# ACT counts the three widest score tiles in the last 12 search rounds of a top-k threshold

## The chip, the cores and the metric

The kernel runs on one core of a Trainium2 chip. The metric is the time of one execution on the device in microseconds (us), for which the slowest core counts; here there is one. The engines are PE (TensorE: matmuls, with PEld for its weight loads), DVE (VectorE), ACT (ScalarE), POOL (GpSimd) and SP (SyncE, which issues the DMAs). Each works through its own queue in the order in which the program wrote it, and they meet at semaphores only.

## What is computed

Two layers of a hybrid trunk, for 1024 prompt tokens and 64 sample tokens. A layer normalises x, projects it through one matrix into all branches, runs a gated linear recurrence (A), a sparse attention (B) and a differential attention (C), gates each, and projects the result back. The change touches how B picks its keys:

```python
s_idx = relu(einsum('bqhd,bkd->bqhk', qi, kidx) * IDX_DIM ** -0.5)
score = einsum('bqhk,bqh->bqk', s_idx, w) * IDX_HEADS ** -0.5
score = where(mask, score, -inf)
top_val, top_idx = top_k(score, 256)        # of up to 1088 keys
# attention B then runs over these 256 keys alone
```

The kernel never sorts. For each query it searches, bit by bit, for the float32 value that at least 256 scores reach, and masks what lies below it.

## The kernel before

Queries are tiled by 128: tiles 0 to 7 are the prompt, tile 8 (SAMPLE) the 64 sample tokens. Prompt tile t sees 128 (t + 1) keys, the sample tile 1088. Tiles 0 and 1 have at most 256 keys and need no selection, so seven tiles are scored (SCORED): 384, 512, 640, 768, 896 and 1024 keys on 128 partitions, and 1088 keys on 64.

A layer has two stages. In the **front**, PE transposes x and runs the input projection in the order of the list FRONT (written by `front()`); it makes the index scores early, and ends with the token-row groups ("tm"): four units (bv, bg, cv, cg) of five groups each, four of the five for 256 tokens and the last for 64, so 20 groups numbered 0 to 19 below. ACT walks the same list and drains every group from PSUM into r_vg (`rows_out`, L1013). The groups use four PSUM banks in turn: PE may fill group n only when group n - 4 has been drained. In the **attention** stage PE, DVE and ACT walk the list STEPS: for each tile and head PE makes scores (L1507 to L1517), DVE reduces them to their maximum (L1298), ACT takes the exponential (L1046), and so on, with two PSUM slots for score maps. The first tile in attention is tile 2, the second the sample tile.

While PE works on the front, DVE does the selection. It has the scores of all seven tiles in SBUF (r_sc), starts from the sign, and then does 31 rounds, one per bit, in `search` (L1225): `count` (L1209) compares each tile with its candidate threshold `cb` and adds up how many scores reach it, one instruction of seven per tile, with the comparison written to r_ix as a by-product; then one small instruction turns the seven counts into a correction (L1229) and one makes the next candidate (L1232, in the last round L1235). The rounds are cut in three pieces of 6, 2 and 23 (SPLITS), with work of the recurrence between them. After round 30 DVE selects: it counts strictly above the threshold (L1268), and then takes four instructions per tile to handle ties and write the mask (L1278 to L1281). The last of them releases `sel_ready`.

Two things wait for that. DVE itself starts with attention only behind it, in its own queue. ACT waits for all seven `sel_ready` (L1034) between its last drain and its first exponential, since the exponentials overwrite r_sc.

Of the kernel before, what the change touches and what calls it, by code (L numbers as in the profile page):

```python
# [6 lines left out]
P = 128  # L7
# [5 lines left out]
SAMPLE = NT - 1  # L13
# [11 lines left out]
TOPK = 256  # L25
# [9 lines left out]
UNITS = ["iq", "ik", "ax0", "ax1", "cq", "bq", "ag0", "ag1", "ck", "bk", "bv", "bg", "cv", "cg"]  # L35
# [28 lines left out]
TMG = [(0, 2), (2, 4), (4, 6), (6, 8), (8, 9)]  # L64
# [11 lines left out]
ORDER = [2, SAMPLE, 3, 0, 1, 4, 5, 6, 7]  # L76
BITS = 31
SPLITS = [6, 2, BITS - 8]


FIRST_PROJ = 3
# [59 lines left out]
def front():  # L141

    def mm(u, s, p):
        return [("mm", u, s, p, k) for k in range(KT)]

    steps = [("xt", 0), ("xt", 1), ("xt", 2)] + mm("iq", 0, 0) + [("xt", 3)] + mm("iq", 1, 0)
    steps += [("xt", 4), ("xt", 5)] + mm("iq", 0, 1) + [("xt", 6), ("xt", 7), ("xt", 8)] + mm("iq", 1, 1)
    steps += mm("iq", 0, 2) + mm("iq", 1, 2)
    for p in range(3):
        steps += mm("ik", 0, p)  # L150

    def after_piece(done):
# [24 lines left out]
    steps.append(("ixr",))  # L177
    todo += [k for u in UNITS[6:10] for s in range(2) for p in range(3) for k in mm(u, s, p)]
    done = 0
    for k in todo:  # L180
        steps.append(k)
        if k[4] < KT - 1:
            continue
        done += 1
        steps += after_piece(done)
    for u in UNITS[10:]:
        for g in range(len(TMG)):
            steps.append(("tm", u, g))
    return steps


# [19 lines left out]
def build(nc, x0, w_in, acst, gate_w, npost, w_out, ckT, kidxT, vcache,  # L211
          y, o_k, o_ik, o_v, o_conv, o_h):
    f32, bf16, i32, u16 = mybir.dt.float32, mybir.dt.bfloat16, mybir.dt.int32, mybir.dt.uint16
    ALU = mybir.AluOpType
# [4 lines left out]
    with ctx:  # L219
# [117 lines left out]
        lamp = sm[:, 216:217]  # L337
        v, smask, cb, kb = smi[:, 0:7], smi[:, 7:14], smi[:, 14:21], smi[:, 21:28]
        bits = sb("bits", 32, i32)
        lamjunk = sb("lamjunk", CHALF)  # L340
        sub2 = sb("sub2", DC)

# [44 lines left out]
        u_ready, h_ready, ya_ready = sem("u_ready"), sem("h_ready"), sem("ya_ready")  # L387
        hl_ready = sem("hl_ready")
        sel_ready = sem("sel_ready")
        lam_s, lam_e, lam_ready = sem("lam_s"), sem("lam_e"), sem("lam_ready")  # L390
        negm_ready, comb_ready = sem("negm_ready"), sem("comb_ready")
        yh_ready, y_ready = sem("yh_ready"), sem("y_ready")
# [168 lines left out]
        for layer in range(DEPTH):  # L561
            x_from = y if layer else x0
            with nc.Block() as block:  # L563
# [315 lines left out]
                def _(act):  # L879
# [122 lines left out]
                    def rows_out(u, g):  # L1002
# [9 lines left out]
                        fn = ACT.Silu if u[1] == "g" else ACT.Copy  # L1012
                        drains_ring(nc.scalar.activation(vg[0:r, t0:t1, c:c + BW], src, fn), key)  # L1013

                    n = 0
                    for s in FRONT:
                        if s[0] == "mm" and s[4] == KT - 1:
                            evac_fm(s[1], s[2], s[3])
                        elif s[0] == "root":
                            act.wait_ge(m2_ready, AJ)  # L1020
                            nc.scalar.activation(tall, tall, ACT.Sqrt, scale=-1.0).then_inc(root_ready, 1)
                        elif s[0] == "iw":
                            weights_out()
                        elif s[0] == "iqs":
                            stack_out(s[1], s[2])
                        elif s[0] in ("ix", "ixr"):
                            relu_out(s, n)
                            n += 1
                        elif s[0] == "ga":
                            gate_out(s[1], s[2], s[3])  # L1030
                        elif s[0] == "tm":
                            rows_out(s[1], s[2])

                    act.wait_ge(sel_ready, len(SCORED))  # L1034
                    nmap = 0
# [39 lines left out]
                def _(dve):  # L1075
                    steps = [0]

                    def link(ins):
                        steps[0] += 1
                        ins.then_inc(dve_step, 1)  # L1080
                        dve.wait_ge(dve_step, steps[0])
# [124 lines left out]

                    def count(bound, last_inc):  # L1209
                        for c, t in enumerate(SCORED):  # L1210
                            b = bound if isinstance(bound, float) else bound[0:rows(t), c:c + 1]
                            ins = vec.tensor_scalar(unsel[t][0:rows(t), :], sc[t][0:rows(t), :], b, None,  # L1212
                                                    ALU.is_ge, ALU.add, accum_out=cnt[0:rows(t), c:c + 1])
                        return ins

                    dve.wait_ge(ik_stored, 16)
# [1 line left out]
                    vec.memset(unsel[SAMPLE][NSA:P, :], 0.0)  # L1218
                    dve.wait_ge(bits_made, 2)
                    link(vec.memset(v, 0))  # L1220
                    link(count(0.0, None))
                    link(vec.tensor_scalar(smask, cnt, float(TOPK), -1.0, ALU.is_lt, ALU.mult))
                    link(vec.scalar_tensor_tensor(cb, v, bits[:, 0:1], smask, ALU.bitwise_or, ALU.bitwise_xor))

                    def search(first, rounds):  # L1225

                        for b in range(first, first + rounds):
                            link(count(cb.bitcast(f32), None))
                            link(vec.tensor_scalar(kb, cnt, float(TOPK), float(2 ** (BITS - 1 - b)),  # L1229
                                                   ALU.is_lt, ALU.mult))  # L1230
                            if b + 1 < BITS:
                                link(vec.scalar_tensor_tensor(cb, kb, bits[:, b + 1:b + 2], cb,  # L1232
                                                              ALU.bitwise_or, ALU.bitwise_xor))
                            else:
                                link(vec.tensor_tensor(cb, cb, kb, ALU.bitwise_xor))  # L1235

                    search(0, SPLITS[0])
                    dve.wait_ge(decay_done, AJ)
# [21 lines left out]
                        vec.tensor_copy(hl[:, j, 0:1], tw[j][:, NPR - 1:NPR])  # L1260
                        ins = vec.tensor_copy(hl[:, j, 1:2], tw[j][:, ACW - 1:ACW])
                    ins.then_inc(hl_ready, 1)
                    search(SPLITS[0] + SPLITS[1], SPLITS[2])

                    thr = cb.bitcast(f32)
                    for c, t in enumerate(SCORED):
# [407 lines left out]
```

## Time and profile before

| | |
|---|---|
| time, median of 3 runs | 1833.22 us (1826.09 to 1840.75) |
| the profiled execution: its own time | 1831.72 us |
| span of its trace | 1829.9 us |
| granted clock of PE, mean over the span | 0.954 |
| busy: PE, DVE, ACT, POOL | 92%, 66%, 31%, 23% of the span |

The span runs from the first to the last instruction of the trace. Layer 0 fills its first half and layer 1 the second; the same work stands 911.2 us later in layer 1. In each layer, the front takes about 487 us from the layer's start and attention the rest. The rows further down are of three kinds: a timeline (start, duration, engine, line, operation, and in brackets how long the engine was idle before it and who released it), groups (all instructions of one line and shape, with count, busy us and mean ns), and windows (how long each engine was busy in a stretch).

### The profile page before, as it was taken

What the parts mean: (1) busy time and instruction counts of PE and PEld (TensorE: products, weight loads), DVE (VectorE), ACT (ScalarE), POOL (GpSimd) and SP (SyncE); (2) the same over time, 40 slices, a digit from 0 to 9 for tenths busy, and PEclk for the clock granted to TensorE, in tenths of its full rate; (3) what the DMA queues carried; (4) which work ended last, traced back from release to release, by engine and by line L of the source; (5) the groups of instructions that cost most, each with busy time, mean ns of one, the idle gap of its engine ahead of it and who ended that gap; (6) DMA issues with size and microseconds to landing.
All of it is one profiled execution on the core that took longest, in us unless ns stands there. A gap on an engine that the chain in (4) does not pass through costs nothing. (4 is left out here: it accounts for less than half of the span.)

```text
span 1829.9 us, 21077 instructions
## 1 busy us (share of the span) xinstructions
PE 1679.8 (92%) x7330; PEld 1125.0 (61%) x7330; DVE 1213.0 (66%) x2510; ACT 568.9 (31%) x1111; POOL 424.6 (23%) x535
## 2 busy tenths in 40 slices
PE   6999999999888989999779999999999888899997
PEld 4566666688745456666345666666887444566663
DVE  3378999999655355565033799999995543456650
ACT  2276421200233223333022864212002332333330
POOL 2001523410022343231110024234000223433211
PEclk9999999999989989999879999999998899899998
DMA  5100001310222021110051000113103120211100
GB/s 163 50 24 24 23 25 60 105 54 24 96 80 104 29 58 35 35 35 24 35 164 49 23 24 23 46 51 94 52 24 127 50 104 29 59 35 35 35 24 35
DMA packets 39177, 99.18 MB, mean 54 GB/s; under 512 B 8673, under 2 KB 27617, under 8 KB 34721
## 3 DMA queue, kind: packets, MB, share of 16 engines
q1 hardware_dynamic: 39072, 97.85, 16.2%
q8 instruction: 59, 0.97, 0.2%
q14 instruction: 46, 0.37, 0.1%
HBM read 66.84 MB, written 18.14 MB: 46 GB/s over the span
## 5 line engine op out<-in xcount | busy, mean ns | idle before, releaser
L1377 PE MATMUL ps<-r_xn,r_w 128*128 128x384 f32 (+1 forms) x1824 | 589.9, 476 | 12.9 <-issue 8.3
L1377 PEld LDWEIGHTS ps<-r_xn,r_w 128*128 128x128 f32 x1824 | 347.3, 192 | 209.9 <-issue 23.2
L1212 DVE TENSOR_SCALAR_CACHE_REDUCE r_ix<-r_sc,smi 128x384 bf16<-128x384 f32 x434 | 405.4, 998 | 2.1
L1298 DVE TENSOR_REDUCE sm<-ps 128x1 f32<-128x384 f32 (+8 forms) x216 | 171.6, 810 | 163.5 <-PE ps L1517 85.9
L1046 ACT ACTIVATE r_sc<-ps,sm 128x384 f32<-128x384 f32 (+8 forms) x216 | 169.8, 787 | 343.8 <-DVE sm L1298 343.3
L1444 PE MATMUL ps<-r_w,r_xn 128*128 128x256 f32 (+1 forms) x1152 | 251.3, 380 | 0.0
L1444 PEld LDWEIGHTS ps<-r_w,r_xn 128*128 128x128 f32 (+1 forms) x1152 | 210.9, 184 | 40.1 <-issue 5.0
L1548 PE MATMUL ps<-r_vg,r_w 128*128 128x64 f32 (+1 forms) x1184 | 162.9, 284 | 26.0 <-DVE r_w L554 14.8
L1548 PEld LDWEIGHTS ps<-r_vg,r_w 128*128 128x128 f32 (+1 forms) x1184 | 151.2, 200 | 35.9 <-DVE r_w L517 21.2
L1531 PE MATMUL ps<-ident,r_sc 128*128 128x128 f32 (+1 forms) x720 | 121.9, 280 | 41.1 <-ACT r_w L517 17.1
L1580 PE MATMUL ps<-r_xn,r_ag 128*128 128x512 f32 (+1 forms) x288 | 146.6, 656 | 8.6 <-DVE r_res L1319 6.1
L1531 PEld LDWEIGHTS ps<-ident,r_sc 128*128 128x128 f32 (+1 forms) x720 | 85.8, 151 | 84.2 <-issue 32.6
L1580 PE MATMUL ps<-r_xn,r_vg 128*128 128x512 f32 (+1 forms) x288 | 130.7, 596 | 0.0
L554 DVE TENSOR_SCALAR r_w<-ps,sm 128x64 f32<-128x64 f32 (+1 forms) x144 | 40.1, 279 | 133.0 <-PE ps L1548 131.8
L1175 DVE SCALAR_TENSOR_TENSOR r_sc<-r_vg,sm,r_sc 128x384 f32<-128x384 f32 (+6 forms) x98 | 97.8, 998 | 30.6 <-ACT r_vg L977 25.0
L1580 PEld LDWEIGHTS ps<-r_xn,r_ag 128*128 128x128 f32 (+1 forms) x288 | 56.3, 205 | 73.6 <-issue 66.7
L977 ACT ACTIVATE r_vg<-ps 128x384 f32<-128x384 f32 (+6 forms) x112 | 88.5, 796 | 31.6 <-PE ps L1414 26.3
L1013 ACT ACTIVATE r_vg<-ps 128x512 f32<-128x512 f32 (+1 forms) x40 | 22.1, 553 | 227.0 <-PE ps L1444 227.0
L517 DVE COPY r_w<-ps 128x512 f32<-128x512 f32 (+3 forms) x112 | 59.7, 533 | 43.7 <-PE ps L1531 42.9
L1511 PE MATMUL ps<-kst_c,qc_hi 128*128 128x512 f32 (+3 forms) x192 | 81.0, 422 | 8.1 <-ACT r_sc L1046 6.5
L1580 PEld LDWEIGHTS ps<-r_xn,r_vg 128*128 128x128 f32 (+1 forms) x288 | 51.3, 185 | 57.5 <-issue 57.2
L517 ACT COPY r_w<-ps 128x512 f32<-128x512 f32 (+3 forms) x112 | 51.6, 461 | 106.7 <-PE ps L1531 106.5
(188 smaller groups left out, 1976.2 us busy)
## 6 DMA issues: line engine op xcount, KB each, us to landing
r_w<-w_in SPq DMA_DIRECT2D x28, 1024.0 KB, 4.9
r_xn<-w_out SPq DMA_DIRECT2D x2, 4096.0 KB, 13.5
y<-r_res SPq DMA_DIRECT2D x16, 512.0 KB, 2.9
r_vg<-x SPq DMA_DIRECT2D x8, 512.0 KB, 9.9
r_xn<-ckT SPq DMA_DIRECT2D x2, 2048.0 KB, 8.4
r_xn<-vcache SPq DMA_DIRECT2D x2, 2048.0 KB, 14.1
o_v<-r_vg SPq DMA_DIRECT2D x4, 1024.0 KB, 11.1
r_sc<-x SPq DMA_DIRECT2D x8, 512.0 KB, 4.4
```

What stands on the lines that cost most here:

```text
L517: ins = copy(pT[i % 2][:, k0:k1, 0:r], src[:, 0:k1 - k0, 0:r])
L977: drains_x(nc.scalar.activation(dst, src, ACT.Relu, scale=scale), key)
L1046: ins = nc.scalar.activation(ex[2 * (i % 2) + m][0:r, 0:w], on_slot(s, w, r), ACT.Exp, bias=negm[0:r, c:c + 1], accum_out=den[0:r, c:c + 1])
L1175: ins = vec.scalar_tensor_tensor(sc[t][0:r, 0:w], src, iw[0:r, t, h:h + 1], sc[t][0:r, 0:w], ALU.mult, ALU.add)
L1212: ins = vec.tensor_scalar(unsel[t][0:rows(t), :], sc[t][0:rows(t), :], b, None, ALU.is_ge, ALU.add, accum_out=cnt[0:rows(t), c:c + 1])
L1298: vec.tensor_reduce(negm[0:r, c:c + 1], on_slot(s, w, r), X, ALU.max, negate=True)\
L1377: ins = nc.tensor.matmul(on_ring(key, cn), w[:, k, P * s + at:P * (s + 1) + at], xnT[:, k, c0:c0 + cn], start=(k == 0), stop=(k == KT - 1))
L1444: ins = nc.tensor.matmul(on_ring(key)[0:rows(t), BW * (t - t0):BW * (t - t0 + 1)], xnT[:, k, P * t:P * t + rows(t)], w[:, k, :], start=(k ...
L1511: ins = nc.tensor.matmul(out, q, kst[kind][:, h, c0:c0 + cn], start=(n2 == 0), stop=(n2 == 1 and not more))
L1531: ins = nc.tensor.transpose(tbank[0:kn, P * (k - 4 * g):P * (k - 4 * g) + r], ex[2 * (i % 2)][0:r, P * k:P * k + kn], ident[0:r, 0:r])
L1548: ins = nc.tensor.matmul(obank[0:r, :], pT[i % 2][0:kn, k, 0:r], vals, start=(k == 0), stop=(k == nk - 1))
L1580: ins = nc.tensor.matmul(mixb[0:r, part // 2, :], yk, wo[:, k, c0:c0 + BANK], start=(k == 0), stop=(k == KT - 1))
```

## The change

In the last 12 rounds (SHARED; rounds 19 to 30) DVE counts only four tiles, those of 384 to 768 keys, and ACT counts the other three (896, 1024 and 1088 keys) with a Sign activation of (candidate - score) whose accumulated output is the number below minus the number above. `limit` holds, for each tile, the bound to which its count is compared. A round now goes to and fro: DVE writes the candidate and raises `cand_ready`; ACT does three passes and raises `act_counted`; DVE, behind its own four counts, waits for them, and makes the next candidate with three small instructions in place of two. Where a score equals the candidate, a sign counts as zero, so ACT's result can be off by one step; `settle` repairs that for the three tiles, once, after round 30: nine small instructions, one exact count of the three tiles on DVE, seven small instructions. The small instructions work on three or six columns.

Where ACT does its counts is set in the list FRONT: `COUNTS_AT` names for each of the 12 shared rounds the token-row group behind whose drain its count stands. One constant table more is filled ahead of the search (11 instructions on DVE with a few columns each), and one copy of the candidates onto themselves raises `cand_ready` for the first time.

```diff
+SHARED = 12
+ACT_TILES = [6, 7, SAMPLE]
+DVE_TILES = [t for t in SCORED if t not in ACT_TILES]
+COUNTS_AT = [5, 6, 7, 7, 8, 9, 9, 10, 11, 11, 12, 13]
...
-    for u in UNITS[10:]:
-        for g in range(len(TMG)):
-            steps.append(("tm", u, g))
+    for n, (u, g) in enumerate([(u, g) for u in UNITS[10:] for g in range(len(TMG))]):
+        steps.append(("tm", u, g))
+        steps += [("count", b) for b, at in enumerate(COUNTS_AT) if at == n]
...
+                    def count_out(b):
+
+                        act.wait_ge(cand_ready, b + 1)
+                        for t in ACT_TILES:
+                            c, r = SCORED.index(t), rows(t)
+                            nc.scalar.activation(unsel[t][0:r, :], sc[t][0:r, :], ACT.Sign, scale=-1.0,
+                                                 bias=cb.bitcast(f32)[0:r, c:c + 1],
+                                                 accum_out=cnt[0:r, c:c + 1]).then_inc(act_counted, 1)
...
+                    def search_shared(first, rounds):
+
+                        for n in range(rounds):
+                            b = first + n
+                            following = float(2 ** (BITS - 2 - b)) if b + 1 < BITS else 0.0
+                            link(count(cb.bitcast(f32), DVE_TILES, ALU.is_lt))
+                            dve.wait_ge(act_counted, len(ACT_TILES) * (n + 1))
+                            link(vec.tensor_tensor(kbf, cnt, limit, ALU.is_gt))
+                            link(vec.tensor_scalar(kb, kbf, float(2 ** (BITS - 1 - b)), following,
+                                                   ALU.mult, ALU.add))
+                            ins = vec.tensor_tensor(cb, cb, kb, ALU.bitwise_xor)
+                            if n + 1 < rounds:
+                                ins.then_inc(cand_ready, 1)
+                                dve.wait_ge(cand_ready, n + 2)
+                            else:
+                                link(ins)
...
+                        link(vec.tensor_tensor(two, high, low, ALU.bitwise_or))
+                        link(vec.tensor_tensor(cb[:, ND:NS], two, sa, ALU.bitwise_xor))
+                        link(count(cb.bitcast(f32), ACT_TILES))
+                        link(vec.tensor_scalar(ca, cnt[:, ND:NS], float(TOPK), -1.0, ALU.is_ge, ALU.mult))
...
-                    search(SPLITS[0] + SPLITS[1], SPLITS[2])
+                    search(SPLITS[0] + SPLITS[1], SPLITS[2] - SHARED)
+                    vec.tensor_tensor(cb, cb, cb, ALU.bitwise_or).then_inc(cand_ready, 1)
+                    dve.wait_ge(cand_ready, 1)
+                    search_shared(BITS - SHARED, SHARED)
+                    settle()
```

**On ACT**, at the drains of token-row groups 4 to 8 of layer 0 (r_vg is where they go, the semaphores in brackets are what each instruction waits for), the queue was, before:

```order
L1013 ACTIVATE r_vg<-ps 64x256 [waits ring_filled1]
L1013 ACTIVATE r_vg<-ps 128x2x256 [waits ring_filled2]
L1013 ACTIVATE r_vg<-ps 128x2x256 [waits ring_filled3]
L1013 ACTIVATE r_vg<-ps 128x2x256 [waits ring_filled0]
L1013 ACTIVATE r_vg<-ps 128x2x256 [waits ring_filled1]
```

Now the first of these places, with the drains of groups 4, 5 and 6:

```order
L1024 ACTIVATE r_vg<-ps 64x256 [waits ring_filled1]
L1024 ACTIVATE r_vg<-ps 128x2x256 [waits ring_filled2]
L1031 ACTIVATE r_ix,sm<-r_sc,smi 128x896 [waits cand_ready]
L1031 ACTIVATE r_ix,sm<-r_sc,smi 128x1024
L1031 ACTIVATE r_ix,sm<-r_sc,smi 64x1088
L1024 ACTIVATE r_vg<-ps 128x2x256 [waits ring_filled3]
```

and the last, from the drain of group 12 (the first row) over that of group 13 (the fifth) to that of group 14:

```order
L1024 ACTIVATE r_vg<-ps 128x2x256 [waits ring_filled1]
L1031 ACTIVATE r_ix,sm<-r_sc,smi 128x896 [waits cand_ready]
L1031 ACTIVATE r_ix,sm<-r_sc,smi 128x1024
L1031 ACTIVATE r_ix,sm<-r_sc,smi 64x1088
L1024 ACTIVATE r_vg<-ps 128x2x256 [waits ring_filled2]
L1031 ACTIVATE r_ix,sm<-r_sc,smi 128x896 [waits cand_ready]
L1031 ACTIVATE r_ix,sm<-r_sc,smi 128x1024
L1031 ACTIVATE r_ix,sm<-r_sc,smi 64x1088
L1024 ACTIVATE r_vg<-ps 64x256 [waits ring_filled3]
```

Between one drain and the next ACT now has one or two counts of three passes each; the first stands behind group 5, the last behind group 13. No instruction between them loads an activation table.

**On DVE**, round 30 and the first instruction of the selection were, before:

```order
L1212 TENSOR_SCALAR r_ix,sm<-r_sc,smi 128x384 [waits dve_step]
L1212 TENSOR_SCALAR r_ix,sm<-r_sc,smi 128x512
L1212 TENSOR_SCALAR r_ix,sm<-r_sc,smi 128x640
L1212 TENSOR_SCALAR r_ix,sm<-r_sc,smi 128x768
L1212 TENSOR_SCALAR r_ix,sm<-r_sc,smi 128x896
L1212 TENSOR_SCALAR r_ix,sm<-r_sc,smi 128x1024
L1212 TENSOR_SCALAR r_ix,sm<-r_sc,smi 64x1088
L1229 TENSOR_SCALAR smi<-sm 128x7 [waits dve_step]
L1235 TENSOR_TENSOR smi<-smi 128x7 [waits dve_step]
L1268 TENSOR_SCALAR r_ix,sm<-r_sc,smi 128x384 [waits dve_step]
```

Now round 30 (its candidate was made by the first row) and the first instruction of the repair are:

```order
L1276 TENSOR_TENSOR smi<-smi 128x7 [waits dve_step]
L1235 TENSOR_SCALAR r_ix,sm<-r_sc,smi 128x384 [waits cand_ready]
L1235 TENSOR_SCALAR r_ix,sm<-r_sc,smi 128x512
L1235 TENSOR_SCALAR r_ix,sm<-r_sc,smi 128x640
L1235 TENSOR_SCALAR r_ix,sm<-r_sc,smi 128x768
L1273 TENSOR_TENSOR sm<-sm 128x7 [waits act_counted,dve_step]
L1274 TENSOR_SCALAR smi<-sm 128x7 [waits dve_step]
L1276 TENSOR_TENSOR smi<-smi 128x7 [waits dve_step]
```

and the repair's count with what stands around it, up to the last small instruction but one ahead of the selection, is:

```order
L1294 ISA sm<-sm 128x6 [waits dve_step]
L1295 TENSOR_TENSOR sm<-sm 128x3 [waits dve_step]
L1296 TENSOR_TENSOR smi<-sm,smi 128x3 [waits dve_step]
L1235 TENSOR_SCALAR r_ix,sm<-r_sc,smi 128x896 [waits dve_step]
L1235 TENSOR_SCALAR r_ix,sm<-r_sc,smi 128x1024
L1235 TENSOR_SCALAR r_ix,sm<-r_sc,smi 64x1088
L1298 TENSOR_SCALAR sm<-sm 128x3 [waits dve_step]
L1299 TENSOR_TENSOR sm<-sm,smi 128x3 [waits dve_step]
L1300 TENSOR_TENSOR sm<-sm 128x3 [waits dve_step]
L1301 TENSOR_TENSOR smi<-smi,sm 128x3 [waits dve_step]
L1302 TENSOR_SCALAR sm<-smi 128x3 [waits dve_step]
L1303 TENSOR_TENSOR smi<-smi,sm 128x3 [waits dve_step]
```

Three counts have left the round; one wait for ACT (`act_counted`) has come into it, and 16 small instructions with one count of three tiles stand between the last round and the selection.

## Rows read from the trace of the kernel before

**Rows 1.** The page, busy us, share and instructions of each engine.

```profile
PE 1679.8 (92%) x7330; PEld 1125.0 (61%) x7330; DVE 1213.0 (66%) x2510; ACT 568.9 (31%) x1111; POOL 424.6 (23%) x535
```

**Rows 2.** Timeline, layer 0: start us, us, engine, line, op [idle before].

```profile
475.82 1.34 DVE L1281 SCALAR_TENSOR_TENSOR r_ix<-r_sc,smi,r_ix 64x1088 bf16<-64x1088 f32 x1
...
487.26 0.41 PE L1511 MATMUL ps<-kst_c,qc_hi 128*128 128x384 f32 x1 [0.76 <-issue]
...
488.02 1.02 DVE L1298 TENSOR_REDUCE sm<-ps 128x1 f32<-128x384 f32 x2 [10.85 <-PE ps L1517]
...
488.65 1.28 ACT L1046 ACT_TABLE_LOAD   x1 [1.74 <-DVE sm L1298]
```

**Rows 3.** Timeline, layer 1, the same places: a V/G drain, DVE's first attention reduce.

```profile
1310.59 0.60 ACT L1013 ACTIVATE r_vg<-ps 128x512 f32<-128x512 f32 x1 [6.73 <-PE ps L1444]
...
1399.21 1.02 DVE L1298 TENSOR_REDUCE sm<-ps 128x1 f32<-128x384 f32 x2 [10.83 <-PE ps L1517]
```

**Rows 4.** Timeline of DVE, layer 0: search rounds, start of the selection.

```profile
353.05 0.61 DVE L1212 TENSOR_SCALAR_CACHE_REDUCE r_ix<-r_sc,smi 128x384 bf16<-128x384 f32 x1
...
427.76 1.14 DVE L1212 TENSOR_SCALAR_CACHE_REDUCE r_ix<-r_sc,smi 128x896 bf16<-128x896 f32 x1
...
431.40 0.17 DVE L1229 TENSOR_SCALAR smi<-sm 128x7 int32<-128x7 f32 x1
...
438.65 0.17 DVE L1235 TENSOR_TENSOR smi<-smi 128x7 int32<-128x7 int32 x1
438.86 0.61 DVE L1268 TENSOR_SCALAR_CACHE_REDUCE r_ix<-r_sc,smi 128x384 bf16<-128x384 f32 x1
```

**Rows 5.** Timeline of ACT, layer 0: drains of three token-row groups.

```profile
399.38 0.60 ACT L1013 ACTIVATE r_vg<-ps 128x512 f32<-128x512 f32 x1 [6.73 <-PE ps L1444]
...
413.19 0.60 ACT L1013 ACTIVATE r_vg<-ps 128x512 f32<-128x512 f32 x1 [6.31 <-PE ps L1444]
...
451.52 0.60 ACT L1013 ACTIVATE r_vg<-ps 128x512 f32<-128x512 f32 x1 [6.31 <-PE ps L1444]
```

**Rows 6.** Groups by line and form: passes of ACT, busy us, mean ns.

```profile
L1046 ACT ACTIVATE r_sc<-ps,sm 64x1088 f32<-64x1088 f32 x24 | 27.9, 1163 | 69.0 <-DVE sm L1298 69.0
L1046 ACT ACTIVATE r_sc<-ps,sm 128x1024 f32<-128x1024 f32 x24 | 26.8, 1115 | 45.2 <-DVE sm L1298 45.2
L1046 ACT ACTIVATE r_sc<-ps,sm 128x896 f32<-128x896 f32 x24 | 24.1, 1008 | 41.6 <-DVE sm L1298 41.6
...
L998 ACT ACTIVATE r_ax<-r_vg,sm 128x1091 f32<-128x1091 f32 x8 | 9.6, 1206 | 0.1
```

**Rows 7.** Timeline of ACT: one pass, its accumulator read, the next pass.

```profile
540.06 1.16 ACT L1046 ACTIVATE r_sc<-ps,sm 64x1088 f32<-64x1088 f32 x1 [0.58 <-DVE sm L1298]
541.12 0.19 ACT L1046 ACTIVATION_READ_ACCUMULATOR r_sc<-ps,sm 64x1 f32 x1
541.22 0.35 ACT L517 COPY r_w<-ps 128x256 f32<-128x256 f32 x1
```

**Rows 8.** Timeline: a DVE reduce and the ACT pass that waits for it.

```profile
502.64 0.55 DVE L1298 TENSOR_REDUCE sm<-ps 128x1 f32<-128x384 f32 x1
...
503.23 0.58 ACT L1046 ACTIVATE r_sc<-ps,sm 128x384 f32<-128x384 f32 x1 [1.42 <-DVE sm L1298]
```

**Rows 9.** Windows: us, busy PE, PEld, DVE, ACT, POOL, PEclk, DMA share, GB/s.

```profile
488.00:500.00 12.00, 8.53 (x40) 6.11 (x39) 7.11 (x22) 5.84 (x15) 1.44 (x2) 0.72 0.77 285
```

**Rows 10.** Timeline of PE inside that window: one score matmul.

```profile
495.93 0.67 PE L1511 MATMUL ps<-kst_c,qc_hi 128*128 128x384 f32 x1
```

**Rows 11.** Sample tile: issue of its cached values, landing (us last), first matmuls.

```profile
491.33 0.44 SPq L642 DMA_DIRECT2D r_xn<-vcache  x1
...
r_xn<-vcache SPq DMA_DIRECT2D x1, 2048.0 KB, 14.1
...
509.71 1.93 PE L1507 MATMUL ps<-r_xn,r_res 128*64 128x512 f32 x4
```

More of the change, by code:

```diff
@@ L78 @@
 SPLITS = [6, 2, BITS - 8]
+SHARED = 12
+ACT_TILES = [6, 7, SAMPLE]
+DVE_TILES = [t for t in SCORED if t not in ACT_TILES]
+ND = len(DVE_TILES)
+NS = len(SCORED)
+COUNTS_AT = [5, 6, 7, 7, 8, 9, 9, 10, 11, 11, 12, 13]
 FIRST_PROJ = 3
@@ L339, in build @@
         bits = sb("bits", 32, i32)
+        limit, kbf, maskf = sm[:, 224:231], sm[:, 231:238], sm[:, 238:241]
+        sti, maski = sm[:, 241:256].bitcast(i32), smi[:, 28:31]
         lamjunk = sb("lamjunk", CHALF)
@@ L389, in build @@
         sel_ready = sem("sel_ready")
+        cand_ready, act_counted = sem("cand_ready"), sem("act_counted")
         lam_s, lam_e, lam_ready = sem("lam_s"), sem("lam_e"), sem("lam_ready")
@@ L1032, in _ @@
                             rows_out(s[1], s[2])
+                        elif s[0] == "count":
+                            count_out(s[1])
                     act.wait_ge(sel_ready, len(SCORED))
@@ L1205, in _, with count @@
                             vec.memset(sc[t][0:64, width(t) - 64:width(t)], LOWEST)
-                    def count(bound, last_inc):
-                        for c, t in enumerate(SCORED):
+                    def count(bound, tiles, op=ALU.is_ge):
+                        for t in tiles:
+                            c = SCORED.index(t)
                             b = bound if isinstance(bound, float) else bound[0:rows(t), c:c + 1]
                             ins = vec.tensor_scalar(unsel[t][0:rows(t), :], sc[t][0:rows(t), :], b, None,
-                                                    ALU.is_ge, ALU.add, accum_out=cnt[0:rows(t), c:c + 1])
+                                                    op, ALU.add, accum_out=cnt[0:rows(t), c:c + 1])
                         return ins
@@ L1220, in _ @@
                     link(vec.memset(v, 0))
-                    link(count(0.0, None))
+                    for c, t in enumerate(SCORED):
+                        vec.memset(limit[:, c:c + 1], float(width(t) - TOPK * (2 if t in ACT_TILES else 1)))
+                    vec.memset(maskf[:, 0:1], 65535.0)
+                    vec.memset(maskf[:, 1:2], 2147418112.0)
+                    link(vec.memset(maskf[:, 2:3], 65536.0))
+                    link(vec.tensor_copy(maski, maskf))
+                    link(count(0.0, SCORED))
                     link(vec.tensor_scalar(smask, cnt, float(TOPK), -1.0, ALU.is_lt, ALU.mult))
@@ L1227, in search @@
                         for b in range(first, first + rounds):
-                            link(count(cb.bitcast(f32), None))
+                            link(count(cb.bitcast(f32), SCORED))
                             link(vec.tensor_scalar(kb, cnt, float(TOPK), float(2 ** (BITS - 1 - b)),
@@ new lines, in settle @@
+                    def settle():
+                        va, sa = v[:, ND:NS], smask[:, ND:NS]
+                        low, high, one, two, ca = (sti[:, 3 * q:3 * q + 3] for q in range(5))
+                        m16, mhi, carry = (maski[:, q:q + 1].to_broadcast([P, 3]) for q in range(3))
+                        link(vec.tensor_tensor(va, cb[:, ND:NS], sa, ALU.bitwise_xor))
+                        link(vec.tensor_tensor(low, va, m16, ALU.bitwise_and))
+                        link(vec.tensor_scalar(low, low, 1.0, None, ALU.add))
+                        link(vec.tensor_tensor(one, low, carry, ALU.bitwise_and))
+                        link(vec.tensor_tensor(low, low, m16, ALU.bitwise_and))
+                        link(vec.tensor_tensor(high, va, mhi, ALU.bitwise_and))
+                        link(vec.tensor_tensor(high, high, one, ALU.add))
+                        link(vec.tensor_tensor(two, high, low, ALU.bitwise_or))
+                        link(vec.tensor_tensor(cb[:, ND:NS], two, sa, ALU.bitwise_xor))
+                        link(count(cb.bitcast(f32), ACT_TILES))
+                        link(vec.tensor_scalar(ca, cnt[:, ND:NS], float(TOPK), -1.0, ALU.is_ge, ALU.mult))
+                        link(vec.tensor_tensor(two, two, va, ALU.bitwise_xor))
+                        link(vec.tensor_tensor(two, two, ca, ALU.bitwise_and))
+                        link(vec.tensor_tensor(va, va, two, ALU.bitwise_xor))
+                        link(vec.tensor_scalar(ca, va, 8388608.0, -1.0, ALU.is_ge, ALU.mult))
+                        link(vec.tensor_tensor(va, va, ca, ALU.bitwise_and))
+                        link(vec.tensor_tensor(cb[:, ND:NS], va, sa, ALU.bitwise_xor))
```

## The prediction

> **What bounds the kernel now.** I read the page first, then the timeline where the front hands over to attention, since the change touches only DVE and ACT in the front. PE is busy for 92% of the span, DVE for 66% [rows 1]. At the hand-over of layer 0 the last instruction of the selection starts at 475.82 and takes 1.34, so DVE is done at 477.16. It then stands idle for 10.85 us: its next work, the first reduce of attention, starts at 488.02, and what released it was PE, which had made its first attention matmul at 487.26 [rows 2]. Layer 1 shows the same with 10.83 us of idleness [rows 3]. So the front ends with PE's last projection group, and the whole search on DVE is hidden behind it, with 10.8 us to spare. A faster search is worth nothing here; a search that ends more than 10.8 us later is paid for in full, because DVE starts attention only behind its selection and ACT's exponentials wait for it too.
>
> **Where the time of a round goes now.** A round is 7.05 us: round 29's first small instruction starts at 431.40, and round 30's 0.21 ahead of its second at 438.65, so at 438.44; the search ends with the latter, and the selection's first count starts at 438.86 [rows 4]. Twelve rounds back, round 19 begins at 353.05 [rows 4]; that is a little more than 12 x 7.05 = 84.6 us before 438.86, since one round on the way was longer. The three tiles that leave DVE are what lies between 427.76 and 431.40, 3.64 us; the four that stay take about 3.0.
>
> **When ACT can count.** This is the step that decides. ACT has time (31% busy), but it works in order, and the first count stands behind the drain of token-row group 5. That drain starts at 399.38, when PE has finished the group [rows 5]. DVE asks for the first count at 353.05 + about 0.2. So DVE does its four tiles by 356.3 and then waits for ACT until about 403.5: some 47 us of idleness, in which the old kernel did more than six rounds. All that the sharing can give back, 12 x (7.05 - 4.2) = 34 us, is less than that.
>
> **The pace from there.** One shared round is ACT's three passes plus the reply. ACT's passes over PSUM with a pointer bias and an accumulator take 1.008, 1.115 and 1.163 us for 896, 1024 and 1088 columns [rows 6]. The new ones read SBUF: the nearest row is L998 with 1.206 us for 1091 columns, 0.04 more than the PSUM form, so I take 1.05 + 1.155 + 1.20 = 3.40. A pass and its successor follow without a gap, and the last accumulator read ends 0.09 behind the pass (541.31 against 541.22) [rows 7]: 3.5 us. A signal from DVE to ACT costs 0.04 (502.64 + 0.55 to 503.23) [rows 8], and I take the same back. DVE's three small instructions are 0.21 each (438.65 to 438.86) [rows 4], 0.6 in all. A round is then 3.5 + 0.6 + 0.08 = 4.2 us. DVE's own 3.0 us lie beside ACT's 3.5. ACT's drains, 0.60 each, fall in the 0.7 us in which it waits for DVE, so they cost nothing; without that cover it would be 0.6 us for each of the six drains on the way.
>
> The counts of rounds 19 to 21 stand alone behind groups 5 to 7, which are 6.9 us apart, so they wait for PE. From the drain of group 7 (413.19 + 0.60 = 413.8) [rows 5] on, rounds chain: round 21's count starts there, round 29's eight rounds later, at 413.8 + 8 x 4.2 = 447.4, and round 30's could at 451.6. It stands behind the drain of group 13, which starts at 451.52 and ends at 452.1 [rows 5]. So the last count runs from 452.1 to 455.6 and the last round ends at 456.3: 17.5 us later than the 438.8 of now. PE isn't held up: no drain is more than about 2 us late, and PE needs a bank again only four groups later. The 11 instructions of the constant table, at most 0.2 us each, delay DVE ahead of a wait of 47 us, and cost nothing.
>
> **The repair and the sum.** `settle` has 16 small instructions at 0.21, 3.4 us, and one count of three tiles, 3.64: 7.0 us, all on the path, since nothing else is on DVE. The selection behind it is unchanged and takes 477.16 - 438.86 = 38.3 us. It ends at 456.3 + 7.0 + 38.3 = 501.6, against 477.16: 24.5 us later. The cover takes 10.85 of it, so attention starts 13.65 us later. On top comes PE's clock. In the window from 488 to 500, after 2 us of idleness, the granted clock is 0.72 on average [rows 9], and a score matmul takes 0.67 us at the lower of the two levels (1.2 GHz) where it took 0.41 at the higher one (2.4 GHz) [rows 10, 2]. With 13 us more of idleness the first maps are made at 1.2 GHz for longer. Eight maps of the first C heads with two such matmuls each would be 4 us if all were exposed; below is nothing, if DVE and ACT hide them. I take 1. In all 14.7 us for a layer, 29 for two, and 1831.7 + 29.3 = 1861 us by the profiled execution's own time, which lies 1.5 us under the median. I predict 1861 us, 1.5% slower.
>
> The Trainium skill speaks against the move itself: "ScalarE: Activation LUTs", section "Rules for kernel authors", would leave simple elementwise work to VectorE, which it calls up to about three times faster per element in bf16. The rows do not show that for this counting: DVE takes 1.14 us for 896 columns [rows 4] and ACT 1.05, so the sum above does not use it. By the rule, with three times DVE's time for the three tiles, a round would be 11.6 us and the kernel about 190 us slower (rival 3).
>
> The same page, section "Table sets: the hidden batching unit", has a function outside the active set cost a table load at each change; the trace has such a load, 1.28 us, ahead of the first exponential [rows 2]. The order of the changed kernel has none between drains and counts, and no term stands for it.
>
> **The rivals.**
> 1. *ACT's place in its queue sets the end of the search* (the forecast): 0.74. 1851 to 1874 us.
> 2. *The round trip is longer than I think.* With the chain of rounds from 413.8 on, each 0.1 us more of a round costs 0.9 us a layer once it passes 4.26. With signals of 0.3 us in place of 0.04, passes of 1.3 us and drains that are not hidden a round would be 5.1 us: the search ends 9 x 5.1 + 0.6 + 3.9 us after 413.8, at 464, and the kernel is at 1831.7 + 2 x (14.7 + 8) = 1877. For it: no row shows an accumulating pass from SBUF with a pointer bias, nor a semaphore that goes to and fro. Against: the rows of both halves are short. 0.14.
> 3. *ACT is far slower per element* than its other passes, as by the rule above: At three times the 3.64 us that DVE takes now for the three tiles a round is 10.9 + 0.7 = 11.6 us, and the 12 rounds chain from 400.0 to 539: 100 us later than now, 96 with the repair and the cover, 2025 us; at twice ACT's 3.4 it is 1930 us. Rows 6 speak against both. 0.02.
> 4. *The cover is enough after all, no change.* The selection would have to end by 488.0, so that the last round ended by 442.7 and ACT's last count began by 438.5. That needs group 13 finished 13 us earlier, or its count not behind it. The order of ACT's queue excludes the second, and PE is busy throughout the first. What could bring it back is something later that waits today for what is not the chain. The sample tile is the first candidate: its cached values are issued at 491.33 and land 14.1 us later, at 505.4, and its first matmuls run at 509.71 with no idleness ahead of them [rows 11]. If that transfer was felt through its traffic, a start 13.7 us later would run undisturbed; I see 4 us of margin and no wait. 1833 us, 0.07.
> 5. *Faster.* The other side: attention gets its 13.7 us back and more, because the transfers (77% DMA share in the window at 488 [rows 9]) are done before it starts, where they slowed it before. It decides only if they cost attention more than 14.7 us a layer, while that window is 12 us long with DVE busy for 7.1. About 1820 us. 0.03.
>
> **How the numbers follow.** The point is that of case 1. The range takes in case 1, with the clock's term from 0 to 4 us a layer and the runs' own spread (1826 to 1841), and reaches to case 2: 1851 to 1877 us. About 1% is what a measurement of this kernel can tell from no change. Slower by over 1% is above 1851.5: nearly all of case 1, and cases 2 and 3, 0.89. Within 1%: 0.08, case 4 and a little of case 1. Faster: 0.03.
>
> **What would show it.** In the changed profile DVE should stand idle for about 47 us in each layer once, behind the four counts of round 19, released by ACT's L1031, and for 2.5 to 3 us in rounds 20 and 21. The rounds from 413.8 on should follow every 4.2 us; if they come every 5, case 2 holds. The last Sign pass should start right behind the drain of group 13, near 452. The first reduce of attention should follow the selection at once, near 501.7, with DVE no longer waiting for PE, and PE idle from 488 to about 504 in its place. PE's projection groups should end at 487 as before; if they end later, drains have held them up, which I exclude. The forecast is wrong if the first reduce starts before 495, or if attention behind it is more than 5 us a layer shorter or longer than before.

## The result: 1.4% slower

| | median us | runs |
|---|---|---|
| before | 1833.04 | 4 (1826.09 to 1840.75) |
| changed | 1857.97 | 4 (1851.01 to 1863.08) |
| ratio | 1.0144 | 95% interval 1.009 to 1.0198 |

The forecast was 1861 us. The profiled execution of the changed kernel took 1851.01 us, the fastest of its four, with a span of 1849.2 us against 1829.9 before.

The page of the changed kernel (busy us, share, instructions), which answers to [rows 1]: ACT has gained 80 us, DVE has lost 69, and the span has grown all the same.

```profile
PE 1674.1 (91%) x7330; PEld 1122.0 (61%) x7330; DVE 1144.2 (62%) x2458; ACT 649.2 (35%) x1255; POOL 427.0 (23%) x535
```

DVE in layer 0 of the changed kernel, timeline (start us, us, engine, line, operation, idleness before it and who ended it). L1273 is the first small instruction of a shared round, L1288 the first of the repair, L1341 the selection's first count, L1354 its last instruction, L1371 the first reduce of attention. It answers to [rows 2] and [rows 4].

```profile
401.57 0.17 DVE L1273 TENSOR_TENSOR sm<-sm 128x7 f32<-128x7 f32 x1 [47.15 <-ACT r_ix L1031]
...
408.48 0.17 DVE L1273 TENSOR_TENSOR sm<-sm 128x7 f32<-128x7 f32 x1 [3.27 <-ACT r_ix L1031]
...
419.55 0.17 DVE L1273 TENSOR_TENSOR sm<-sm 128x7 f32<-128x7 f32 x1 [0.54 <-ACT r_ix L1031]
...
448.69 0.17 DVE L1273 TENSOR_TENSOR sm<-sm 128x7 f32<-128x7 f32 x1 [0.53 <-ACT r_ix L1031]
...
453.71 0.17 DVE L1273 TENSOR_TENSOR sm<-sm 128x7 f32<-128x7 f32 x1 [1.40 <-ACT r_ix L1031]
...
454.32 0.16 DVE L1288 TENSOR_TENSOR smi<-smi 128x3 int32<-128x3 int32 x1
...
461.14 0.61 DVE L1341 TENSOR_SCALAR_CACHE_REDUCE r_ix<-r_sc,smi 128x384 bf16<-128x384 f32 x1
...
498.95 1.34 DVE L1354 SCALAR_TENSOR_TENSOR r_ix<-r_sc,smi,r_ix 64x1088 bf16<-64x1088 f32 x1
500.33 1.02 DVE L1371 TENSOR_REDUCE sm<-ps 128x1 f32<-128x384 f32 x2
```

The whole course stands here. DVE is idle for 47.15 us (46.07 in layer 1) before it can finish the first shared round, waiting for ACT. In rounds 20 and 21 it waits for 3.3 us, in the eight after them for 0.53 each, and in the last for 1.40. The last round ends at 454.3, the repair at 461.1, the selection at 500.3, and the reduce of attention follows at once, with no idleness ahead of it, where DVE waited for 10.85 us before [rows 2].

ACT in the same layer, timeline: L1024 are drains (groups 5, 13 and 19), L1031 the passes of the new counts, and ACTIVATION_READ_ACCUMULATOR what each pass has behind it. It answers to [rows 5] and [rows 6].

```profile
397.54 0.60 ACT L1024 ACTIVATE r_vg<-ps 128x512 f32<-128x512 f32 x1 [6.73 <-PE ps L1517]
398.03 1.03 ACT L1031 ACTIVATE r_ix<-r_sc,smi 128x896 bf16<-128x896 f32 x1
...
399.06 1.14 ACT L1031 ACTIVATE r_ix<-r_sc,smi 128x1024 bf16<-128x1024 f32 x1
...
400.19 1.19 ACT L1031 ACTIVATE r_ix<-r_sc,smi 64x1088 bf16<-64x1088 f32 x1
401.28 0.19 ACT L1031 ACTIVATION_READ_ACCUMULATOR r_ix<-r_sc,smi 64x1 f32 x1
...
449.68 0.60 ACT L1024 ACTIVATE r_vg<-ps 128x512 f32<-128x512 f32 x1 [1.09 <-PE ps L1517]
450.17 1.03 ACT L1031 ACTIVATE r_ix<-r_sc,smi 128x896 bf16<-128x896 f32 x1
...
484.70 0.38 ACT L1024 ACTIVATE r_vg<-ps 64x256 f32<-64x256 f32 x1 [3.00 <-PE ps L1517]
```

ACT drained group 5 at 397.54 and began its first count within that drain's end; the last count starts behind the drain of group 13. This execution's front ran 1.84 us ahead of the one before (last drain 484.70 against 486.54), so every absolute time of layer 0 is to be read with 1.84 us added: the first reduce at 500.33 answers to 502.17, and the forecast said 501.7.

PE, timeline: the first matmul of attention, and the first that had to wait for an exponential.

```profile
485.42 0.42 PE L1584 MATMUL ps<-kst_c,qc_hi 128*128 128x384 f32 x1 [0.76 <-issue]
...
502.99 0.69 PE L1584 MATMUL ps<-kst_c,qc_hi 128*128 128x384 f32 x1 [16.44 <-ACT r_sc L1068]
```

PE is where it was at the end of the front, and then has nothing to do for 16.44 us (2.3 us before).

The distance from the last drain of the front to the first reduce of attention doesn't depend on how fast the front ran. It is 1.48 and 1.46 us in the two layers of before and 15.63 and 15.63 in the changed kernel: 14.16 us later per layer, 28.3 in all, against 26.4 by the ratio (16.5 to 36 by its interval). All experiments below are read by this distance, called **the gap**. It is steadier than the time: the two layers of one kernel agree within 0.04 us, while the runs of one kernel spread over 7 to 23 us.

### The profile page after: what moved, and what is told of

Same layout as the page of the kernel before. It is cut to its first block and busy times, and to the rows that moved or that the text cites. A ratio compares the mean times of both kernels' runs of the same rounds, so it can differ in the third digit from the quotient of the medians.

```text
span 1849.2 us, 21193 instructions
## 1 busy us (share of the span) xinstructions
PE 1674.1 (91%) x7330; PEld 1122.0 (61%) x7330; DVE 1144.2 (62%) x2458; ACT 649.2 (35%) x1255; POOL 427.0 (23%) x535
## 5 line engine op out<-in xcount | busy, mean ns | idle before, releaser
L1235 DVE TENSOR_SCALAR_CACHE_REDUCE r_ix<-r_sc,smi 128x768 bf16<-128x768 f32 (+6 forms) x368 | 328.0, 953 | 2.2
L1371 DVE TENSOR_REDUCE sm<-ps 128x1 f32<-128x384 f32 (+8 forms) x216 | 171.6, 810 | 137.6 <-PE ps L1590 63.1
L1653 PE MATMUL ps<-r_xn,r_ag 128*128 128x512 f32 (+1 forms) x288 | 141.6, 638 | 7.3 <-DVE r_res L1392 6.1
L1031 ACT ACTIVATE r_ix<-r_sc,smi 128x896 bf16<-128x896 f32 (+2 forms) x72 | 80.5, 1120 | 7.0 <-DVE smi L1276 7.0
```

The lines of the kernel that those rows point to most:

```text
L1371: vec.tensor_reduce(negm[0:r, c:c + 1], on_slot(s, w, r), X, ALU.max, negate=True)\
L1653: ins = nc.tensor.matmul(mixb[0:r, part // 2, :], yk, wo[:, k, c0:c0 + BANK], start=(k == 0), stop=(k == KT - 1))
```

## The experiments

They are called e1 (counts moved forward), e2 (moved back), e3 (six shared rounds), e4 (no repair), e5, e6 and e7 (one, three and six counts added on DVE), e9 (e1 with three counts added) and e8 (POOL held back). Every ratio is to the kernel before, run beside it.

**Theory A** is the forecast's: the front ends with PE, the search is hidden behind it, and what the changed kernel loses comes from where its counts stand in ACT's queue (behind groups 5 to 13), plus the repair, less the cover of 10.85 us. **Theory B**: sharing itself costs, through handshakes, the repair and late drains, wherever the counts stand. **Theory C**: a search that ends earlier gains something.

### The counts moved forward

```diff
-COUNTS_AT = [5, 6, 7, 7, 8, 9, 9, 10, 11, 11, 12, 13]
+COUNTS_AT = [0, 0, 1, 2, 2, 3, 4, 4, 5, 6, 6, 7]
```

> The changed kernel with its 12 counts on ACT moved forward in ACT's queue (COUNTS_AT from 0,0,1,2,2,3,4,4,5,6,6,7), nothing else. Theory A, the place sets the end: the first count can run at about 367 us in place of 398, the 12 rounds chain at 4.16 us, the search ends near 420, repair and selection near 465, DVE then waits some 21 us for PE, and the time is that of the kernel before: 1833 us, ratio 1.00 (0.995 to 1.005). Theory B, the sharing itself costs (handshakes, repair, ACT late with its drains), wherever it stands: again about 1858 us. Theory C, a search that ends earlier is worth something after all: clearly below 1833 us, with 21 us of cover in each layer.

Measured: 1833.63 us, ratio 1.0011 (0.9989 to 1.0033). DVE's timeline in layer 0, its first, second and last shared round and the first reduce:

```profile
372.50 0.44 DVE L1273 TENSOR_TENSOR sm<-sm 128x7 f32<-128x7 f32 x1 [15.73 <-ACT r_ix L1031]
377.34 0.17 DVE L1273 TENSOR_TENSOR sm<-sm 128x7 f32<-128x7 f32 x1 [0.53 <-ACT r_ix L1031]
...
419.61 0.17 DVE L1273 TENSOR_TENSOR sm<-sm 128x7 f32<-128x7 f32 x1 [0.53 <-ACT r_ix L1031]
...
488.50 1.02 DVE L1371 TENSOR_REDUCE sm<-ps 128x1 f32<-128x384 f32 x2 [23.16 <-PE ps L1590]
```

Same instructions, same handshakes, same repair, and no cost: B is refuted. The 12 rounds chain at 4.16 us and DVE then stands idle for 23.16 us before PE is done. These 23 us per layer buy nothing that could be seen (the interval reaches down to 0.9989, 2 us): C is refuted too. The first wait is 15.7 us even here, since the first count stands behind the drain of group 0, and DVE asks some 15 us before ACT has done it.

### The counts moved back

```diff
-COUNTS_AT = [5, 6, 7, 7, 8, 9, 9, 10, 11, 11, 12, 13]
+COUNTS_AT = [7, 8, 9, 9, 10, 11, 11, 12, 13, 13, 14, 15]
```

> The changed kernel with its counts moved back by two token-row groups (COUNTS_AT from 7 to 15). The last count stands behind group 15, whose drain starts 10.7 us later than that of group 13 (462.22 against 451.52 in the profile of before). Theory A: the first reduce of attention comes 10.6 us later in each layer than in the changed kernel, +21 us, 1879 us, ratio to before 1.026. Theory B: where they stand does not matter, 1858 us. If what comes later in attention gives such delays back, less than +21.

Measured: 1881.28 us, ratio 1.0274 (1.024 to 1.0308). The gap is 27.99 and 27.98 us, 12.4 more than in the changed kernel, where 10.6 was expected. The expectation named the wrong group: two counts stand behind group 13 now, one behind 14 and one behind 15, and these four chain. ACT starts them at 453.5, 457.68, 461.84 and 466.00; the last could have started near 464 behind group 15's matmuls, and waits for the chain. Twice the 26.5 us by which the gap exceeds that of before is 53; the ratio gives 50. The waits of DVE on ACT in layer 0 (us in total, times, longest):

```profile
DVE sm L1273 <- ACT r_ix L1031: 71.8, 12, 61.0
```

### Half as many shared rounds

```diff
-SHARED = 12
+SHARED = 6
-COUNTS_AT = [5, 6, 7, 7, 8, 9, 9, 10, 11, 11, 12, 13]
+COUNTS_AT = [5, 5, 6, 7, 7, 8]
```

> The changed kernel with 6 shared rounds in place of 12 (SHARED = 6) and the first count still behind group 5 (COUNTS_AT 5, 5, 6, 7, 7, 8). DVE comes to the first shared round at about 395 us, ACT to its count at 399, so the wait of 47 us is gone, and the rounds chain to about 426; with repair and selection DVE is done near 471, before PE's 487. Theory A: 1833 us, ratio 1.00. Theory B: half of the cost of the rounds and all of the repair stay, about 1845 to 1850 us.

Measured: 1832.16 us, ratio 1.0004 (0.9978 to 1.003). The waits of DVE on ACT in layer 0, and the first reduce:

```profile
DVE sm L1273 <- ACT r_ix L1031: 7.6, 6, 3.6
486.15 1.02 DVE L1371 TENSOR_REDUCE sm<-ps 128x1 f32<-128x384 f32 x2 [16.73 <-PE ps L1590]
```

With the first count at the very same place, behind group 5, six shared rounds cost nothing, because DVE comes there when ACT does: 7.6 us of waiting in six rounds, where the changed kernel has 59.3 us in the twelve of its layer 0 and 117.6 in both layers. The last count stands behind group 8 here, so a late place of the last count is out of the way too.

```profile
DVE sm L1273 <- ACT r_ix L1031: 117.6, 24, 47.1
```

### Without the repair

```diff
-                    settle()
```

> The changed kernel without the repair behind the last round (no call of settle: the thresholds of the three widest tiles can be one step off). The repair took 6.8 us in layer 0 of the changed kernel (454.32 to 461.14), and nothing covers it if the selection is the last to end. Theory A: 2 x 6.8 = 13.6 us less than the changed kernel, 1844 us, ratio to before 1.006 to 1.009. If the delay of attention were not what costs, no difference from 1858 us.

Measured: 1847.58 us, ratio 1.0089 (1.0056 to 1.0122), 10 us less than the changed kernel's median. The gap is 8.77 us in both layers, 6.86 less. Over the kernel before it is 14.6 us for two layers; the ratio gives 16. So the repair is on the path with its full length, once the selection is last. The gap shows this; the intervals of the two ratios (1.0056 to 1.0122 here, 1.009 to 1.0198 for the changed kernel) overlap.

### How long the cover is: counts added on DVE

To the kernel before, behind the last round, with 1, 3 and 6 for K:

```diff
+                    for _ in range(K):
+                        link(count(cb.bitcast(f32), None))
```

> The kernel before with one count of all seven tiles more behind the last round, on DVE alone (6.6 us a layer: 424.82 to 431.40), whose result is what the last round's count would be for the final threshold and is overwritten. It measures the cover of 10.85 us. Theory A: all of it is hidden, DVE's idleness ahead of the first reduce falls to 4.2 us, time 1833 us, ratio 1.00. If DVE's end mattered already: +13 us, ratio 1.007.

Measured: 1828.84 us, ratio 0.9994 (0.9972 to 1.0016). DVE's first reduce, layer 0:

```profile
487.50 1.02 DVE L1300 TENSOR_REDUCE sm<-ps 128x1 f32<-128x384 f32 x2 [4.25 <-PE ps L1519]
```

In layer 1, 3.16 us are left.

> The kernel before with three such counts, 19.7 us a layer. Theory A: 19.7 - 10.85 = 8.9 us come out in each layer, +18 us, 1851 us, ratio 1.010; with the low clock of PE behind its idleness costing 1 us a layer, +20. The clock alone at its most (4 us a layer) would give +26.

Measured: 1854.03 us, ratio 1.0128 (1.0097 to 1.0158), which is 23 us; the gap is 11.16 and 11.20 us.

> The kernel before with six such counts, 39.5 us a layer. Theory A: 28.6 us come out in each layer, +57 us, 1890 us, ratio 1.031, plus what the clock costs, which should be no more than with three, since PE's idleness is beyond the change of its clock in both. If attention gave part of a delay back, the step from three to six counts would be less than 2 x 19.7 = 39.5 us.

Measured: 1887.46 us, ratio 1.0309 (1.0275 to 1.0344), which is 57 us; the gap is 30.87 us in both layers.

With no count on ACT at all, the same law holds. The gap grows by 0, by 9.7 and by 29.4 us with 6.6, 19.7 and 39.5 us of work: that is the work less 10.8 us of cover, with 0.8 us on top in the last two, whose selection takes 39.0 to 39.1 us in place of 38.3 (on this more below). Twice these are 0, 19.4 and 58.8 us; the ratios give -1, 23 and 57. Three counts cost a little more than the gap says (17.8 to 29 us by the interval, so this is not resolved).

### What the sharing is worth where it is early

The kernel of the first experiment with three such counts behind the repair (K = 3, as above).

> The counts on ACT moved forward as in e1, and three more counts of all seven tiles on DVE (19.7 us a layer) behind the repair. In e1 DVE stood idle for 23.16 us ahead of the first reduce. If what the sharing gives is cover and nothing else, these 19.7 us are hidden, the idleness falls to 3.4 us, and the time is that of the kernel before, 1831 us, ratio 1.00, where the same three counts cost 1.0128 in the kernel before (e6). If the cover of e1 were only apparent, +18 to +24 us.

Measured: 1829.68 us, ratio 1.0009 (0.999 to 1.0028), where the same counts took the kernel before to 1.0128. DVE's first reduce, layer 0:

```profile
488.83 1.02 DVE L1373 TENSOR_REDUCE sm<-ps 128x1 f32<-128x384 f32 x2 [3.42 <-PE ps L1592]
```

So the sharing does free DVE for 19.7 us a layer, if it stands early; this kernel has nothing to put there.

### Who stretched the selection

The selection takes 38.3 us in the kernel before and 39.2 in the changed one. The instructions that grew run while POOL prepares the B queries of the first tile. POOL and DVE of the changed kernel, timelines (two casts and two subtractions on POOL; for the 1024-key tile L1351 and L1352 on DVE):

```profile
485.23 1.60 POOL L833 CAST qb_hi<-r_qk 64x256 fp32r<-64x256 f32 x2 [113.08 <-ACT r_vg L1024]
486.91 2.57 POOL L838 TENSOR_TENSOR qb_lo<-r_qk,qb_hi 64x256 fp32r<-64x256 f32 x2
...
487.81 1.10 DVE L1351 TENSOR_SCALAR r_ix<-r_sc,smi 128x1024 bf16<-128x1024 f32 x1
488.94 2.69 DVE L1352 TENSOR_TENSOR_SCAN r_ix<-r_ix 128x1024 uint16<-128x1024 bf16 x1
```

The same two instructions of DVE in the kernel before:

```profile
465.42 0.75 DVE L1278 TENSOR_SCALAR r_ix<-r_sc,smi 128x1024 bf16<-128x1024 f32 x1
466.21 2.29 DVE L1279 TENSOR_TENSOR_SCAN r_ix<-r_ix 128x1024 uint16<-128x1024 bf16 x1
```

To test it, POOL's part was held back until the selection was done:

```diff
                     tokens_ready(pool)
+                    pool.wait_ge(sel_ready, len(SCORED))
                     pad_b(0)
```

> The changed kernel with POOL's four instructions for the first tile's B queries (pad_b(0), at 485 to 489.5 us in layer 0) held back until the selection is done. In the changed kernel the selection takes 39.2 us (461.14 to 500.33) where it took 38.3 before, and three DVE instructions that lie in the same microseconds as POOL's are the ones that grew. If the two slow each other down, the selection takes 38.3 us again here and the first reduce stands 14.8 us behind the last drain in place of 15.6, and POOL's casts take 0.85 us in place of 1.60. If something else stretched the selection (its place behind PE's end), it stays at 39.2. The time as a whole can't tell 1.7 us; one look.

Measured in a single run: 1863.96 us; the gap is 14.78 and 14.80 us in place of 15.63. DVE and POOL, timelines of layer 0:

```profile
491.13 0.75 DVE L1352 TENSOR_SCALAR r_ix<-r_sc,smi 128x1024 bf16<-128x1024 f32 x1
491.92 2.29 DVE L1353 TENSOR_TENSOR_SCAN r_ix<-r_ix 128x1024 uint16<-128x1024 bf16 x1
...
502.90 0.56 DVE L1372 TENSOR_REDUCE sm<-ps 128x1 f32<-128x384 f32 x1
...
503.03 0.85 POOL L833 CAST qb_hi<-r_qk 64x256 fp32r<-64x256 f32 x2 [127.46 <-DVE r_ix L1355]
503.96 1.52 POOL L838 TENSOR_TENSOR qb_lo<-r_qk,qb_hi 64x256 fp32r<-64x256 f32 x2
```

DVE's instructions are back at 0.75 and 2.29 us, and POOL's pairs take 0.85 and 1.52 us in place of 1.60 and 2.57. They slow each other down, and it costs 0.85 us a layer. Not every instruction of DVE suffers alike: the two that ran beside POOL's casts and the start of its subtractions went from 1.15 to 1.23 and 1.17 us only, while the casts took nearly twice as long. In the kernel before, the casts fell into DVE's idleness and the subtractions beside its first reduce of attention, which reads PSUM, and neither side was longer (0.85, 1.52 and 1.02 us).

## Why the prediction held, point by point

- **Bound and cover.** Right. The cover was read as 10.85 us, and e5 to e7 show it: 6.6 us of extra work disappear, and of 19.7 and 39.5 us all that goes beyond the cover comes out.
- **The first count.** Right: 47.15 us of idleness against 47 forecast, with the rounds 20 and 21 at 3.3 against 2.5 to 3 us.
- **The pace.** A chained round takes 4.17 us (423.71 to 427.88 in the trace) against 4.2. ACT's passes are 1.03, 1.14 and 1.19 us against 1.05, 1.155 and 1.20; DVE waits 0.53 us behind its own four counts. That rules out rival 2. The near tie between the chain and group 13 went as said: ACT waited for PE once more, and the last count began at 450.17, behind the drain of group 13. But this place costs little: DVE waits 1.40 us there in place of 0.53, so 0.87 of the loss belongs to it. Nearly all of the rest comes from the start: rounds 19 to 21 wait for groups 5 to 7, and nine more rounds at 4.17 us follow. No run moved the first or the last count alone.
- **PE's groups.** Right that they aren't held up: from the drain of group 5 to the last drain it is 87.16 us in both kernels. The drains are up to 2.9 us late (group 10: 431.85, or 433.69 with the 1.84 us added, against 430.80), where about 2 was the most expected.
- **The repair.** 6.82 us (454.32 to 461.14) against 7.0, and e4 shows that all of it counted.
- **The selection.** Taken as unchanged, and 0.85 us longer. This is the one thing on the path that the sum did not have: it asked what is queued behind DVE, and not what else would run in the microseconds into which DVE's work was moved.
- **The clock.** Wrong as a term, though small. In the windows of the changed kernel (us, busy PE, PEld, DVE, ACT, POOL, granted clock, DMA share, GB/s) it is at the lower level throughout the first 12 us of attention in layer 0:

```profile
486.00:500.00 14.00, 0.55 (x5) 0.26 (x3) 13.68 (x10) 0.00 (x0) 3.33 (x3) 0.66 0.66 246
500.00:512.00 12.00, 8.44 (x32) 6.30 (x32) 7.10 (x23) 5.83 (x15) 0.00 (x0) 0.50 1.01 353
```

That is 0.50 (1.2 GHz) in place of the 0.72 in [rows 9], which is a mean over both levels. Yet the added low clock costs nothing. From the first reduce to the first matmul of the sample tile it is 21.7 and 24.2 us in the two layers of before, and 24.1 and 21.7 in the changed kernel. Over the ten layers in which DVE had idleness left (before, e1, e3, e5, e9) the mean is 22.8 us, and over the twelve in which PE stood idle for 9.6 to 31.7 us ahead of attention (changed, e2, e4, e6, e7, e8) it is 22.7.

What goes with the length of this stretch is when the clock comes back to the higher level, counted from the first reduce. Here are the windows from 10.7 to 20.7 us behind it, layers 0 and 1 of the kernel before, and then of the changed one:

```profile
498.72:508.72 10.00, 8.00 (x52) 5.97 (x53) 7.49 (x27) 4.05 (x13) 3.02 (x7) 1.00 1.02 354
1409.91:1419.91 10.00, 9.85 (x39) 7.99 (x39) 5.86 (x19) 3.54 (x11) 1.24 (x4) 0.50 1.03 361
```

```profile
511.03:521.03 10.00, 9.85 (x39) 7.99 (x39) 5.85 (x19) 3.53 (x11) 1.23 (x4) 0.50 0.11 43
1429.66:1439.66 10.00, 8.02 (x52) 5.97 (x53) 7.48 (x27) 4.04 (x12) 3.01 (x7) 1.00 0.09 37
```

Where the clock is back by then, the stretch takes 21.7 us; where it is low to the end of the window, 24.2 and 24.1. All 22 layers follow this: with the clock back after 9.5 to 10.7 us the stretch takes 21.7 us, after 14.4 to 15.6 it takes 22.8, after 19.4 it takes 23.9, and after 21 it takes 24.1 to 24.2. The start of the low clock doesn't matter: it falls 4 us behind the first reduce in layer 0 of before and some 10 us ahead of it in layer 1 of the changed kernel, and both take 21.7. The delay brings the start forward and doesn't move the end later (14.5 us on average in the twelve layers, 15.4 in the ten), so it adds nothing. A clock that comes back at 21 and not at 10 us goes with 2.5 us more, in either kernel. That it causes them is read from PE, busy for 9.85 of the 10 us at the lower level and for 8.0 at the higher, and not tested; why the end falls where it does, no run here separates. I took 1 us a layer for the delay; it is 0.
- **The sum.** 13.65 + 1 = 14.65 us a layer were forecast. The trace has 13.65 - 0.14 (last round) - 0.18 (repair) + 0.85 (selection) = 14.18, and the gap gives 14.16. The two errors of mechanism, an added low clock that costs nothing (1 us too much) and a collision with POOL that does cost (0.85 us left out), nearly cancel. That the sum came within 0.5 us a layer is in this part luck; the waits, the pace, the repair and the cover are not.
- **Given back later.** Rivals 4 and 5 needed attention to be shorter. From the first reduce to the layer's last row (DVE's multiplication ahead of the last store) it is 419.7 and 423.2 us before, 414.0 and 422.7 in the changed kernel, and 418.6 to 423.6 in all of e2, e4, e6, e7 and e8. The means are 421.1 us over the twelve delayed layers and 420.5 over the ten others, so no giving back can be seen. Taken by the letter, the sign that the forecast set for itself (attention more than 5 us shorter or longer) did appear, in layer 0 of the changed kernel, 5.7 us shorter. It was set too narrow: e1 shows one such layer too (415.2), with no delay at all, and the same stretch differs by 3.5 us between the layers of the kernel before. The profiled execution (1851 us) is the shortest of its four in part because of that layer. Traffic doesn't bring anything back either: the two windows above with the clock at 1.00 have a DMA share of 1.02 and 0.09, nearly the same work in them, and stretches of 21.7 us both.

The rule that leaves simple elementwise work to VectorE ("ScalarE: Activation LUTs", "Rules for kernel authors" of the Trainium skill) gives its factor of about three for bf16, and these scores are float32. For this form the trace shows no such advantage: ACT's pass over 1024 columns with an accumulator takes 1.14 us and lets the next one start after 1.13, where DVE's count of the same tile in the repair takes 1.28 and lets the next one start after 1.20 (457.17 to 458.37). The other rule, that a function outside the active set costs a load ("Table sets: the hidden batching unit", same page of the Trainium skill), agrees with the trace as far as it goes: no load stands between drains and counts in either layer, and the first exponential behind them has one (1.28 us).

No kernel here is faster than the kernel before. What limits the layer at this point is PE's front, and the versions that remove the loss (e1, e3) are only as fast as before.

## What to carry to other kernels

When work is moved to an engine that seems to have time, its place in that engine's queue decides, and not the share of its busy time: find the instruction behind which it stands, read when that one ends, and compare it with the time when the result is first asked for. Then ask whether the engine that is relieved was on the path at all: DVE worked through the search without a break and still had 10.85 us of idleness behind it, so there was nothing to gain, and everything beyond 10.85 us to lose. When a chain of rounds hangs on such places, look at the first of them before the last: here the rounds took 4.17 us each from the moment they could chain, and the last place cost 0.87 us. Last, look at what already runs in the microseconds into which work is pushed.

## What the hardware showed

- The round trip between DVE and ACT over semaphores is short here. A loop of 4.17 us holds 3.46 us of three ACT passes with their accumulator read and 0.58 us of three small DVE instructions; what is left for the two signals is 0.03 us from DVE to ACT and 0.10 back.
- DVE and POOL slowed each other down where both worked in SBUF: a 128 x 1024 comparison took 1.10 in place of 0.75 us, a scan 2.69 in place of 2.29, POOL's pair of casts 1.60 in place of 0.85, and its pair of subtractions 2.57 in place of 1.52. Beside DVE's reduce from PSUM, the subtractions took their 1.52.
- PE's idleness of 9.6 to 31.7 us ahead of a stage in which DVE and ACT take turns with it had no price that could be seen: it brought the fall of the clock to 1.2 GHz forward, and the stage's first 22 to 24 us were no longer for it. What they did vary with was the moment at which the clock came back: 21.7 us long with 9.5 to 10.7 us of the stage gone by then, 22.8 with 14.4 to 15.6, 24.2 with 21.
